# Four edits ahead of the expert stage: grouped normalisation, a third weight set, gate rows through DRAM, backward end keys first

## The reference, cut to what matters

```
mod = silu(c) @ w_mod + b_mod            # six vectors of 1024: shift1, scale1, gate1, shift2, scale2, gate2
h   = rmsnorm(x, g_pre_mix) * (1 + scale1) + shift1
z   = h @ w_in                           # split into q, k, v, r, a_fwd, a_bwd, p
log_a = log_sigmoid(a @ w_alpha + b) / 16       # forward and backward decays, chunks of 64 tokens
o   = gla(q, k, v, log_a_fwd) + flip(gla(flip(...), strict=True))   # k_end = k * exp(b_last - b), u = k_end^T v
o   = rmsnorm(o) * silu(r)
pool: for windows 2, 4, 8, 16: (centred mean - token) @ w_pool[group] * pool_scale
x   = x + gate1 * rmsnorm(concat(o, pool) @ w_out, g_post_mix)
x   = x + gate2 * rmsnorm(experts(...), g_post_ffn)
```

## Time and profile before

| | us |
|---|---|
| median of 3 runs | 3079.92 |
| lowest and highest | 3058.76, 3092.85 |
| the profiled execution, its own time | 3087.5 |
| its span in the trace | 3085.7 |
| PE busy in the span | 2877.9 (93%) |
| DVE, ACT, POOL busy | 2153.1, 1253.1, 1311.1 |

### The profile page before, as it was taken

One profiled execution on the slowest core, in us unless ns is written; L12 is line 12 of the kernel. 1 busy time (PEld: TensorE's weight loads), 2 busy tenths in 40 slices (PEclk: granted clock), 3 DMA queues, 4 the chain that ended last, 5 costly groups with the idle time before them and its releaser, 6 DMA issues.

```text
span 3085.7 us, 43263 instructions
## 1 busy us (share of the span) xinstructions
PE 2877.9 (93%) x15980; PEld 2607.5 (85%) x15980; DVE 2153.1 (70%) x3694; ACT 1253.1 (41%) x2311; POOL 1311.1 (42%) x1038
## 2 busy tenths in 40 slices
PE   5997999999999999799999988998999999999997
PEld 4785778899999999799998978888898887887776
DVE  5545536896588786478787856655566887887877
ACT  5323552233377676343443423433432222332222
POOL 0002100000000002467776756565667888888882
PEclk9998999999999999899998978988999999999999
DMA  6510222235556655678887867777789999999996
GB/s 258 207 56 28 91 111 71 67 121 180 179 196 207 207 196 186 198 258 294 272 299 247 307 222 250 233 253 240 263 278 356 354 354 332 366 350 338 339 349 222
DMA packets 326206, 720.29 MB, mean 233 GB/s; under 512 B 41920, under 2 KB 157760, under 8 KB 324288
## 3 DMA queue, kind: packets, MB, share of 16 engines
q1 hardware_dynamic: 235968, 450.12, 41.9%
q0 software_dynamic: 90112, 268.76, 25.8%
HBM read 604.45 MB, written 114.29 MB: 233 GB/s over the span
## 4 chain that ended last, share of the span: by engine, by line
PE 57%; POOL 16%; issue 7%; DVE 2%; DMA 1%; ACT 1%; SPq 1%; DVEq 0%; ACTq 0%; POOLq 0%
PE mix L1412 47%; POOL picked_act L1838 8%; POOL rows L1845 8%; PE mix L112 5%; PE sps_all L1880 2%; PE sps_all L1898 1%; PE mix L1898 1%; ACT onehot L1611 1%; PE sps_all L1497 1%; DVE lo L102 0%; DMA rows<-in_v,eidx 0%; SPq L1377 0%; DMA act_in<-act_late 0%; DMA wq_raw<-in_w_q 0%; DVE onehot L1690 0%
## 5 line engine op out<-in xcount | busy, mean ns | idle before, releaser
L1838 POOL DMA_INDIRECT picked_act<-act_early,aidx x384 | 456.9, 1190 | 988.0 <-DMA act_early<-gelu 871.2
L1412 PE MATMUL mix<-a_hi,hi 128*128 128x320 f32 (+1 forms) x3072 | 837.3, 326 | 31.8 <-issue 29.1
L1412 PE MATMUL mix<-a_hi,lo 128*128 128x320 f32 (+1 forms) x3072 | 834.9, 325 | 33.0 <-issue 32.6
L1412 PE MATMUL mix<-a_lo,hi 128*128 128x320 f32 (+1 forms) x3072 | 835.0, 325 | 32.9 <-issue 32.1
L102 DVE TENSOR_TENSOR lo<-raw,hi 128x1024 fp32r<-128x1024 f32 x384 | 469.3, 1222 | 546.9 <-ACT hi L97 484.7
L1845 POOL DMA_INDIRECT rows<-in_v,eidx x512 | 650.6, 1271 | 392.2 <-DVE ys L1749 223.6
L1749 DVE SCALAR_TENSOR_TENSOR ys<-rows,coef,ys 128x1024 f32<-128x1024 f32 x504 | 629.3, 1282 | 64.2 <-DMA rows<-in_v,eidx 53.7
L1412 PEld LDWEIGHTS mix<-a_hi,hi 128*128 128x128 f32 x3072 | 553.6, 194 | 46.5 <-issue 42.5
L1412 PEld LDWEIGHTS mix<-a_lo,hi 128*128 128x128 f32 x3072 | 553.4, 194 | 46.0 <-issue 45.4
L1412 PEld LDWEIGHTS mix<-a_hi,lo 128*128 128x128 f32 x3072 | 553.1, 194 | 40.9 <-issue 40.7
L97 ACT ACTIVATE hi<-raw 128x1024 fp32r<-128x1024 f32 x384 | 404.7, 1054 | 410.6 <-PE mix L1898 366.8
(11 more groups left out here) (267 smaller groups left out, 3928.8 us busy)
## 6 DMA issues: line engine op xcount, KB each, us to landing
raw<-in_u SPq DMA_DIRECT2D x256, 512.0 KB
raw<-in_v SPq DMA_DIRECT2D x128, 512.0 KB
act_late<-gelu SPq DMA_DIRECT2D x128, 320.0 KB
act_in<-act_late SPq DMA_DIRECT2D x128, 256.0 KB
act_early<-gelu SPq DMA_DIRECT2D x128, 192.0 KB
gate_d<-free_lo SPq DMA_DIRECT2D x19, 1024.0 KB
gt<-gate_d SPq DMA_DIRECT2D x64, 256.0 KB
free_lo<-gate_d SPq DMA_DIRECT2D x64, 256.0 KB
```

The lines of the kernel that those rows point to most:

```text
L1412: done = pe.matmul(dst, w, a[:, k, cols], start=first, stop=last)
L1838: pool.indirect_dma_start(out=g.picked_act[:, e:e + 1], out_offset=None, in_=act_tables[e // (EARLY * CHOSEN)], in_offset=bass.IndirectOff ...
```

## The change

- *Opening.* Tokens are squared and normalised in three groups of 3, 3 and 2 tiles: DVE squares the first tile of each group, ScalarE the others, ScalarE takes a root per group, DVE does all normalising. PE starts turn(0) group by group. consts and vecs are loaded ahead of w_mod(0). Each chunk's columns are finished alone, and a_hi(k) waits for its own columns.
- *Projections.* A third set of split weights, at the addresses of x(6) and x(7), holds tile 2, and its split on ScalarE no longer waits for PE. w_alpha is issued ahead of the wait for the last a_lo and of w_mod_b.
- *Gate rows.* The gate columns are stored to DRAM as 2048 single elements, and loaded back as one row broadcast to all partitions; spread, make_rows and the copies go.
- *Pooling.* pool_product stands ahead of value tiles 1, 3, 4 and 6, none behind tile 7.
- *Attention.* Backward end keys come first; forward and backward token keys change places in SBUF; gamma is made on ScalarE behind the SiLU in the stage before.

```diff
...
-XN_SPLIT = 5
-COLS_AFTER = (1, 2, 3, 3, 4, 4, 5, 5)
+XN_GROUPS = ((0, 1, 2), (3, 4, 5), (6, 7))
...
+        g.gate_rows_d = nc.dram_tensor("gate_rows_d", (1, 2 * D), F32, kind="Internal").ap()
...
-    g.w_hi = [g.at(f"w_hi{s}", 76 + 4 * s, [P, D], F32R) for s in range(2)]
-    g.w_lo = [g.at(f"w_lo{s}", 84 + 4 * s, [P, D], F32R) for s in range(2)]
+    g.w_hi = [g.at(f"w_hi{s}", kb, [P, D], F32R) for s, kb in enumerate((76, 80, 24))]
+    g.w_lo = [g.at(f"w_lo{s}", kb, [P, D], F32R) for s, kb in enumerate((84, 88, 28))]
...
+        sp.dma_start(g.consts[:], i["consts"]).then_inc(consts_in, 16)
+        sp.dma_start(g.vecs[:], i["vecs"]).then_inc(vecs_in, 16)
         load_columns(0)
-        sp.dma_start(g.vecs[:], i["vecs"]).then_inc(vecs_in, 16)
-        sp.dma_start(g.consts[:], i["consts"]).then_inc(consts_in, 16)
...
-        for t in range(TT):
-            act.wait_ge(x_in[t], 16)
-            if t:
-                act.wait_ge(ssq_ready, t)
-            act.activation(junk[:], x[:, t, :], ACT.Square, accum_out=g.ssq[:, t:t + 1]).then_inc(ssq_ready, 1)
-        act.wait_ge(ssq_ready, TT)
-        act.wait_ge(eps_ready, 1)
-        act.activation(g.rstd[:, 0:TT], g.ssq[:, 0:TT], ACT.Sqrt, scale=1.0 / D, bias=g.eps[:]).then_inc(root_ready, 1)
-        act.wait_ge(rstd_ready, 1)
-        for t in range(XN_SPLIT):
-            last = act.activation(x[:, t, :], x[:, t, :], ACT.Copy, scale=g.rstd[:, t:t + 1])
-        last.then_inc(xn_ready, 1)
+        squares = 0
+        for n, tiles in enumerate(XN_GROUPS):
+            for t in tiles[1:]:
+                act.wait_ge(x_in[t], 16)
+                if squares:
+                    act.wait_ge(ssq_ready, squares)
+                act.activation(junk[:], x[:, t, :], ACT.Square, accum_out=g.ssq[:, t:t + 1]).then_inc(ssq_ready, 1)
+                squares += 1
+            act.wait_ge(ssq_ready, squares)
+            act.wait_ge(squares_ready, n + 1)
+            act.wait_ge(eps_ready, 1)
+            cols = slice(tiles[0], tiles[-1] + 1)
+            act.activation(g.rstd[:, cols], g.ssq[:, cols], ACT.Sqrt, scale=1.0 / D, bias=g.eps[:]).then_inc(root_ready, 1)
...
-            act.wait_ge(cols_ready, COLS_AFTER[k])
+            act.wait_ge(cols_ready, k + 1)
...
+        def finish_columns(k):
+            dve.tensor_scalar(g.mod[:, k:k + 1], g.mod[:, k:k + 1], g.vec("b_mod")[:, k:k + 1], None, ALU.add)
+            dve.tensor_scalar(g.scale1[:, k:k + 1], g.mod[:, KC + k:KC + k + 1], shift_scale[:, k:k + 1],
+                              g.vec("g_pre_mix")[:, k:k + 1], ALU.add, ALU.mult).then_inc(cols_ready, 1)
...
+        def square(n):
+            t = XN_GROUPS[n][0]
+            dve.wait_ge(x_in[t], 16)
+            dve.scalar_tensor_tensor(junk_v[n][:], x[:, t, :], 1.0, x[:, t, :], ALU.mult, ALU.mult,
+                                     accum_out=g.ssq[:, t:t + 1]).then_inc(squares_ready, 1)
+
+        def normalize(n):
+            tiles = XN_GROUPS[n]
+            cols = slice(tiles[0], tiles[-1] + 1)
+            dve.wait_ge(root_ready, n + 1)
+            dve.reciprocal(g.rstd[:, cols], g.rstd[:, cols]).then_inc(rstd_ready, 1)
+            dve.wait_ge(rstd_ready, n + 1)
+            for t in tiles:
+                last = dve.tensor_scalar(x[:, t, :], x[:, t, :], g.rstd[:, t:t + 1], None, ALU.mult)
+            last.then_inc(xn_ready, 1)
+
+        square(0)
+        square(1)
+        normalize(0)
+        square(2)
+        normalize(1)
+        normalize(2)
+        dve.wait_ge(vecs_in, 16)
+        dve.tensor_scalar(shift_scale[:], g.vec("b_mod")[:, KC:2 * KC], 1.0, None, ALU.add)
...
         dve.wait_ge(silu_ready, 1)
         columns(0)
+        finish_columns(0)
+        columns(1)
+        finish_columns(1)
         weights_low(0)
         low(0)
         columns(2)
+        finish_columns(2)
         weights_low(1)
         low(1)
+        for k in range(3, KC):
+            columns(k)
+            finish_columns(k)
+            low(k - 1)
+        low(KC - 1)
...
+                if k == 0 and t in starts:
+                    pe.wait_ge(xn_ready, starts[t] + 1)
...
-    POOL_AT = {2: 0, 4: 1, 6: 2}
-    ROWS_AT = {4: 0, 6: 1, 7: 2}
-    mod_done, spread_ready, rows_ps, rows_ready = (sem(n) for n in (
-        "mod_b_done", "spread_ready", "rows_ps", "rows_ready"))
+    POOL_AT = {1: 0, 3: 1, 4: 2, 6: 3}
...
+        weights_at = lambda n: 2 if n == 2 else n % 2
...
+            sp.dma_start(w_alpha[:], i["w_alpha"]).then_inc(w_alpha_in, 16)
             sp.wait_ge(g.a_lo_ready, KC)
             load_columns(0)
-            sp.dma_start(w_alpha[:], i["w_alpha"]).then_inc(w_alpha_in, 16)
...
+            sp.wait_ge(gate_cols_ready, 1)
+            columns = g.gate_rows_d.rearrange("a (n p) -> (a p) n", p=P)
+            sp.dma_start(columns, g.gate_cols[:], allow_slow_non_contiguous=True).then_inc(rows_stored, 16)
+            sp.wait_ge(rows_stored, 16)
+            sp.dma_start(flat(g.gate_rows[:]), g.gate_rows_d.to_broadcast([P, 2 * D])).then_inc(rows_in, 16)
+            sp.wait_ge(rows_in, 16)
...
-                act.wait_ge(tile_done, n - 1)
-                split_hi(act, w_hi[n % 2][:], raw[n % 2][:]).then_inc(hi_ready, 1)
+                if n > 2:
+                    act.wait_ge(tile_done, n - 1)
+                split_hi(act, w_hi[weights_at(n)][:], raw[n % 2][:]).then_inc(hi_ready, 1)
...
+            for d in range(2):
+                for pair in range(PAIRS):
+                    ends = g.prefix[d][:, pair, :].rearrange("p (n c) -> p n c", c=CHUNK)[:, :, CHUNK - 1:CHUNK]
+                    act.activation(g.gamma[:, d, pair, :], ends.squeeze(2), ACT.Exp, scale=1.0 / TAU)
...
-            pool_group_out(3)
...
-            def gate_row(n):
-                gate = g.gate_cols[:, n * half:(n + 1) * half]
-
-                dve.tensor_copy(spread[:], gate.unsqueeze(2).to_broadcast([P, half, P])).then_inc(spread_ready, 1)
-                dve.wait_ge(rows_ps, n + 1)
-                dve.tensor_copy(g.gate_rows[:, n // 2, n % 2 * HALF:(n % 2 + 1) * HALF], rows).then_inc(rows_ready, 1)
+            dve.tensor_tensor(g.gate_cols[:, KC:], g.mod[:, 5 * KC:6 * KC], g.vec("g_post_ffn"), ALU.mult)\
+               .then_inc(gate_cols_ready, 1)
...
                 pool_group(n, w)
-                if n:
-                    gate_row(n - 1)
-            gate_row(3)
...
-            pool_product(3)
-            make_rows(3)
...
+END_ORDER = (1, 0)
...
-    k_tok = [g.at(f"k_tok{d}", (177, 136)[d], [P, TT, PAIRS * P]) for d in range(2)]
+    k_tok = [g.at(f"k_tok{d}", (160, 177)[d], [P, TT, PAIRS * P]) for d in range(2)]
...
+            def tail(pair):
                 total = last_of(prefix[0], pair).to_broadcast([P, NCHUNK, CHUNK])
                 dve.tensor_tensor(chunks(e_end[0], pair), total, chunks(prefix[0], pair), ALU.subtract).then_inc(tail_ready, 1)
+
+            def end_keys(d, pair):
+                dve.wait_ge(end_exp, END_ORDER.index(d) * PAIRS + pair + 1)
+                dve.tensor_tensor(g.k_end[d][:, pair, :], g.z[:, 2 + pair, :], e_end[d][:, pair, :], ALU.mult)\
+                   .then_inc(k_end_done, 1)
+
+            tail(0)
             dve.wait_ge(ones_ready, 1)
-            for d in range(2):
-                for pair in range(PAIRS):
-                    dve.wait_ge(end_exp, d * PAIRS + pair + 1)
-                    dve.tensor_tensor(g.k_end[d][:, pair, :], g.z[:, 2 + pair, :], e_end[d][:, pair, :], ALU.mult)\
-                       .then_inc(k_end_done, 1)
+            end_keys(1, 0)
+            tail(1)
+            end_keys(1, 1)
+            end_keys(0, 0)
+            end_keys(0, 1)
...
-            dve.wait_ge(gamma_ready, 1)
...
         @block.scalar
         def _(act):
             for pair in range(PAIRS):
+                act.activation(chunks(e_end[1], pair)[:, :, 1:], chunks(prefix[1], pair)[:, :, :CHUNK - 1], ACT.Exp,
+                               scale=1.0 / TAU).then_inc(end_exp, 1)
+            for pair in range(PAIRS):
                 act.wait_ge(tail_ready, pair + 1)
                 act.activation(e_end[0][:, pair, :], e_end[0][:, pair, :], ACT.Exp, scale=1.0 / TAU).then_inc(end_exp, 1)
-            for pair in range(PAIRS):
-                act.activation(chunks(e_end[1], pair)[:, :, 1:], chunks(prefix[1], pair)[:, :, :CHUNK - 1], ACT.Exp,
-                               scale=1.0 / TAU).then_inc(end_exp, 1)
-            for d in range(2):
-                for pair in range(PAIRS):
-                    last = act.activation(g.gamma[:, d, pair, :], last_of(prefix[d], pair).squeeze(2), ACT.Exp, scale=1.0 / TAU)
-            last.then_inc(gamma_ready, 1)
...
-                if d:
+                if d == END_ORDER[1]:
...
```

More of the change, by code:

```diff
@@ L183, in modulation @@
     junk = g.at("junk_a", 112, [P, D])
+    junk_v = [g.at(f"junk_a{n}", 160 + 4 * n, [P, D]) for n in range(len(XN_GROUPS))]
+    shift_scale = g.at("scale_bias", 195.25, [P, KC])
     g.silu_row = g.at("silu_row", 124, [P, D])
```

(51 more changed lines are left out.)

22 lines of the change are left out of this document (7 added, 15 removed).

## The result

The changed kernel takes 3070.89 us (median of 20 runs, 3046.93 to 3095.45), the kernel before 3091.48 (20 runs, 3058.76 to 3107.99); the ratio is 0.9949, 95% interval 0.9928 to 0.9971. On 3091.48 that is 15.8 us less (9.0 to 22.3); the medians alone differ by 20.6. The profiled execution of after has a span of 3062.0 against the one in the earlier trace rows.

The account below looks back on a forecast made before the run. TensorE (PE) was taken to bound the kernel, so its gaps before mark 330 count. 2.1+10.2+7.8+0.5 = 20.6 us off the profiled 3087.5 gave 3067; runs' median 7.6 lower, so 3059, range 3034 to 3081.

Parts of the forecast that it names:

- End keys: Start of attention: table load gone, first product 1.3 us earlier, PE's transposed groups start earlier; gain 0.5, up to 2.0.
- Range and chances: Whole kernel: 3034 to 3081 us; faster by over 1% 0.24, slower by over 1% 0.03, the rest 0.73.
- (a): Rival behind mark 330: a DMA limit there swallows the shift, gain not passed on; 3070 to 3080 us, chance 0.12.
- (d): Rival at the end of the projections: gate-column store makes the kernel slower, 3131 us at 1 us per element; chance 0.03.
- Opening: Opening products up to the wait for w_alpha: PE ends them earlier; gain 2.1 us, between 1.0 and 3.7.
- the charge of 1.6: Opening: PE's first work in short pieces runs at lower clock; 1.6 us taken off the gain, possible 0 to 2.7.
- Third set and w_alpha: Projections to tile 2: w_alpha's wait and the half clock go; gain 10.2 us (9.5 to 10.3), third set some 0.7.
- Value tiles: Value tiles to block end: make_rows and its wait go, a new 2.0 us pooling wait comes; gain 7.8 (5.1 to 7.8).
- Gate rows: Gate rows via DRAM: store of 3 to 38 us and load hidden under 60.7 us of cover; gain 0.
- (b): Rival: full clock in both doubtful places and end keys at their best; gain 23.8, 3056 us, chance 0.2.
- (c): Rival: the clock falls in both doubtful places; gain 16.1, 3064 us, chance 0.15.
- (e): Rival at the value tiles: first pooled map takes until 209, costing 3 us more; counted in the range, no own chance.

Follow-up runs that it names:

- third_set_alone: Kernel before with only the third pair of split-weight buffers and its index added, w_alpha's load where it was; one execution, span 3058.8 us.
- w_alpha_early: Kernel before with only w_alpha's load issued ahead of SP's wait for the last a_lo; 3077.13 us against 3077.24, ratio 1.0007 (0.9969 to 1.0044).
- end_keys_forward: Changed kernel with forward end keys first again, at the old addresses and in the old order on DVE and ScalarE; one execution, span 3043.9 us.
- store_15_times: Changed kernel with the gate-column store and its wait done fifteen times in a row, on chip 13; 2975.47 us against 2864.89.
- store_28_times: Changed kernel with the gate-column store and its wait done twenty-eight times in a row, on chip 13; 3112.83 us against 2864.89.
- after_third: Changed kernel, unchanged, timed a third time, on chip 13; 2864.89 us against 2883.63 for the kernel before, ratio 0.9933 (0.9916 to 0.9951).
- two_weight_sets: Changed kernel with two sets of split weights and the wait for tile_done 1 again, w_alpha still early; one execution, span 3045.5 us.

## Why the prediction was right or wrong

**The time.** 3059, between 3034 and 3081, for 3070.9. The difference that it rests on, 20.6, was 20.9 at the last mark ahead of the dense products, and 19.3 and 15.8 by the ratios of the times. The mechanism was right in the opening, in w_alpha's load and in the value tiles but for the clock; the parts measured sum to 2.4+10.0+5.8+1.2 = 19.4 at the first score (291.30-271.93), and 21.2 at the dense products. That this comes so near to 20.6 is in part luck: the value tiles gave 2.0 less than forecast, and what made up for it are 0.7 at the first score that no experiment ties to an edit (see End keys), and 1.8 between the first score and the dense products, in code that no edit touches. That the medians too are 20.6 apart is luck as well: the ratio says 15.8.

**The step that failed** is the one in "Range and chances": *"before spans 3058.8 to 3092.9, and 1% is 30.8 us, about what a measurement of this kernel can tell from none."* I set the spread of single runs against the gain and made a change that can't be told likeliest (0.73). What tells is the interval of the ratio over many runs: with 20 a side it is 0.22% to either side, and 0.25% for a kernel against itself (12 against 28). 20.6 us are 0.67%, three times that. By my own sum, of whose cases only (a), at 0.12, and (d), at 0.03, gained less than 16 us (0.5%), a gain that can be told had 0.85, though one of over 1% stayed unlikely. The second fault of that step: I centred the forecast on the median of three runs, 3079.9; that of twenty is 3091.5. 11.6 of the 11.9 us by which I forecast too low are this.

**Opening, 2.1 (1.0 to 3.7): 2.4.** First logit 58.09 where PE was ready for it at 60.46; other profiles of the same opening have PE ready at 57.59 to 59.33, so 1.1 to 2.9. Landing times and groups came as stepped: consts at 15.89 for 16, DVE done with the tiles at 18.95 for 19.4, a_hi(0) at 21.89 for 22.3; the last low part came at 54.4 for 53.4, and PE did not wait for it. In after PE's first products ran at half rate from 27.40 to about 35 (1.22 and 1.05 for a pair, 0.62 later), of which the part from 31.29 is the charge of 1.6. The granted clock in the view is 1.00 over 16 to 31 and 31 to 57 us all the same, so this loss is seen in the lengths of the products and not in that column. In my text the transposes are said to gain 4.3; by its own times for the end of turn(0), 19.8 and 25.7, it is 5.9, and 4.3 is the gain at their last group's start. The 3.4 at a_hi(0), on which the sum rests, doesn't depend on it. Which of the groups, the single columns and the early consts gave the 2.4 was not tried.

**Third set and w_alpha, 10.2: 10.0** (the second logit 12.4 earlier, less the 2.4). The set's 0.7 was the 0.85 of wait; that the clock can fall behind it, 1.6 more, wasn't in my sum.

**Value tiles, 7.8 (5.1 to 7.8): 5.8.** The part became 163.74-157.96 long. The new wait was put at 2.0 and was 2.27. The term that was mis-sized is the clock behind it: taken at 0, it cost 1.7. I had ranked the wait by its length between one of 1.8 that did not drop the clock and one of 3.5 that did. Its length doesn't decide it: the same 2.3 dropped the clock in four profiles of eight, and the 3.5 itself did not in one of five (third_set_alone).

**Gate rows, 0:** hidden. The store took 12.0, between my 3 and 38, and would have been seen from 56; rival (d) falls. The Trainium skill, DMA: Bandwidth & Descriptors (Specifications), has pieces under 512 bytes handled with a read-modify-write. The trace agrees so far as 8 KB in 2048 pieces take 12.0 us where edges' 32 KB in 128 pieces take 2.4; but both kinds of piece are under 512 bytes, and no run here isolates the read-modify-write.

**End keys, 0.5: not shown.** Attention's start to the first score is 1.2 shorter (29.84 for 31.03), but the forward order has 29.87. The means, 30.65 of five profiles with before's front and 30.07 of ten with after's, differ by 0.6, less than either kind scatters (29.95 to 31.03, 29.00 to 30.72). What differs between executions of one order is how long PE's transposes run at half clock: until about 9.7 us after attention's start in before, until about 6.4 in w_alpha_early. I read PE's idle time ahead of attention and took that length as unchanged. The 1.3 that I gave to the vanished table load are the order's: end_keys_forward, without that load too, has its first product 2.42 after attention's start as before has (after: 1.15).

**Rivals.** (a), not passed on, falls by store_15_times and store_28_times on chip 13. On the other chips, whose dense products pause, only the times of the change speak: 15.8 us (9.0 to 22.3) and 12.3 (2.5 to 21.9) allow the whole 20.9, but also a part of it. (b) and (c), the clock in both doubtful places: profiles of one program have one and the other at the pooling wait, so they are executions rather than cases. (e) didn't occur: the wait was 2.3.

**Open.** Why PE pauses, and the clock is lower, in the dense products on some chips. Whether a shift arrives whole on those chips too. Whether w_alpha_early's time holds the 7 to 12 us of its marks. What decides whether the clock falls behind a given wait.

## What to carry to other kernels

Judge whether a gain can be told by the interval of paired runs, not by the spread of single ones, and read its size at a mark just behind the edited part, where profiles repeat to 1 or 2 us. A wait bought to shorten an order costs twice if the clock falls behind it: here one product a tile later costs nothing that the marks show and saves 2.5 to 4.2 us. Before you put a price on what follows a wait, read several profiles of the same program. When a buffer and a load are moved together, do each alone: here one was worth 7.5 or more, the other 0.85 to 2.5 and only behind the first.

## What was not expected of the hardware

The same program takes 2864.9 us on one chip (13) and 3072.5 on another (11), with the granted clock from 1300 to 2100 us 1.00 in after_third against 0.93 to 0.94 in after, and 102.6 us of PE's pauses without a releaser in the latter; up to about 1200 us the profiles are equal. Behind a wait of 0.85 us the clock fell in w_alpha_early and not in two_weight_sets; behind one of 2.3 us it fell to 0.50 in four profiles of eight, two executions of one program among them that differ; behind one of 3.5 us it fell in four of five. In after's opening the products ran at half rate (1.05 to 1.22 us a pair for 0.62) in a stretch whose granted clock reads 1.00. A store of 128x16 elements of 4 bytes costs 10.9 to 12.0 us, first or sixth alike, and 11.0 on average over 28 in a row.
